# Delta-rule inverse by levels: three of its six product levels multiply four diagonal blocks of 32 by 32 in place of two of 64 by 64

## The reference

```python
kb = k * beta[..., None]
lower = jnp.where(strict, jnp.einsum('nbhcd,nbhsd->nbhcs', kb, k) * decay, 0.0)
eye = jnp.eye(C, dtype=jnp.float32)                       # C = 64
rhs = jnp.concatenate([v * beta[..., None], kb * jnp.exp(gc)[..., None]], axis=-1)
sol = lax.linalg.triangular_solve(eye + lower, rhs, left_side=True, lower=True,
                                  unit_diagonal=True)
```

## Time and profile before

| | us |
|---|---|
| median of the runs (lowest, highest) | 2251.85 (2248.36, 2258.47) |
| the profiled execution, its own time | 2253.49 |
| its span, first instruction to last | 2251.7 |
| TensorE matmul busy | 2146.6 (95%) |
| VectorE busy | 1097.8 (49%) |
| ScalarE busy | 752.4 (33%) |
| mean granted TensorE clock | 0.977 of full |
| the levels of group 0 | about 244 to 276 |
| the levels of group 1 | about 304 to 348 |

### The profile page before, as it was taken

The page is one execution under the profiler, slowest core; times in us unless marked ns, Lnnn a source line. Parts: engine busy times, 40 slices in busy tenths (PEclk is TensorE's granted clock), DMA queues, the critical chain, the costliest instruction groups (busy, mean ns, idle before and its releaser), DMA issues.

```text
span 2251.7 us, 28790 instructions
## 1 busy us (share of the span) xinstructions
PE 2146.6 (95%) x11831; PEld 1757.9 (78%) x11831; DVE 1097.8 (49%) x1381; ACT 752.4 (33%) x1038; POOL 155.3 (7%) x137
## 2 busy tenths in 40 slices
PE   7999999899999999999999999899789999999998
PEld 6877888788888778767788888687469868888886
DVE  4664654454354353452744435555745334454453
ACT  5443432422122232673312213312435243222222
POOL 2000220200000210001100000300001001000001
PEclk9999999999999999999999999999889999999999
DMA  6231000122222222102222222322104302222221
GB/s 233 75 115 45 22 11 15 70 100 98 93 93 93 94 75 75 38 1 75 75 94 105 99 94 93 122 94 75 38 20 143 119 20 94 94 94 99 106 93 56
DMA packets 27025, 182.81 MB, mean 81 GB/s; under 512 B 2992, under 2 KB 3120, under 8 KB 5424
## 3 DMA queue, kind: packets, MB, share of 16 engines
q1 hardware_dynamic: 25200, 174.07, 21.8%
q10 hardware_dynamic: 1296, 4.71, 0.5%
q0 software_dynamic: 432, 2.62, 0.3%
HBM read 179.30 MB, written 2.10 MB: 81 GB/s over the span
## 4 chain that ended last, share of the span: by engine, by line
PE 86%; DVE 8%; ACT 3%; DMA 1%; issue 1%; POOL 0%; ACTq 0%; DVEq 0%; POOLq 0%; SPq 0%
PE PS L472 85%; ACT Y L1254 2%; DVE HL L1888 2%; DVE Y L1888 1%; DVE PS L1888 1%; DVE XT L1891 1%; DVE WL L1891 1%; ACT WH L1254 1%; DVE Y L1891 1%; DMA MX<-mem_t 0%; DVE SQ L1891 0%; PE PS L1070 0%; DMA STG<-weights 0%; PE PS L641 0%; POOL SQA L412 0%
## 5 line engine op out<-in xcount | busy, mean ns | idle before, releaser
L472 PE MATMUL PS<-HH,WH 128*128 128x512 f32 x1608 | 643.0, 400 | 32.4 <-DVE HL L1888 26.0
L472 PE MATMUL PS<-HL,WH 128*128 128x512 f32 x1608 | 632.1, 393 | 0.0
L472 PE MATMUL PS<-HH,WL 128*128 128x512 f32 x1608 | 631.6, 393 | 0.0
L1891 DVE TENSOR_TENSOR WL<-STG,WH 128x2048 fp32r<-128x2048 f32 (+1 forms) x167 | 376.3, 2253 | 286.5 <-ACT WH L1254 286.5
L1254 ACT ACTIVATE WH<-STG 128x2048 fp32r<-128x2048 f32 (+1 forms) x167 | 313.9, 1880 | 529.3 <-PE PS L472 527.8
L472 PEld LDWEIGHTS PS<-HH,WH 128*128 128x128 f32 x1608 | 305.4, 190 | 112.5 <-issue 28.7
L472 PEld LDWEIGHTS PS<-HH,WL 128*128 128x128 f32 x1608 | 305.4, 190 | 65.2
L472 PEld LDWEIGHTS PS<-HL,WH 128*128 128x128 f32 x1608 | 305.8, 190 | 62.7 <-issue 1.7
L472 PE MATMUL PS<-UPH,WH 128*128 128x512 f32 x768 | 299.1, 389 | 1.4 <-DVE UPL L1888 1.4
L472 PE MATMUL PS<-UPL,WH 128*128 128x512 f32 x768 | 298.8, 389 | 0.0
L472 PE MATMUL PS<-UPH,WL 128*128 128x512 f32 x768 | 298.8, 389 | 0.0
(11 more groups left out here) (291 smaller groups left out, 2127.2 us busy)
## 6 DMA issues: line engine op xcount, KB each, us to landing
STG<-weights SPq DMA_DIRECT2D x163, 1024.0 KB, 4.8
XT<-x_t ACTq DMA_DIRECT2D x2, 1024.0 KB, 12.4
out_t<-Y SPq DMA_DIRECT2D x8, 256.0 KB, 2.0
STG<-weights SPq DMA_DIRECT2D x4, 256.0 KB, 5.7
MX<-mem_t ACTq DMA_DIRECT2D x4, 256.0 KB, 8.3
CON<-consts ACTq DMA_DIRECT2D x1, 1024.0 KB, 17.2
Y<-recip_counts POOLq DMA_DIRECT2D x1, 1024.0 KB, 5.1
KVM<-mem_t POOLq DMA_DIRECT2D x1, 1024.0 KB, 7.2
```

Source lines behind the costliest of these rows:

```text
L472: return pe.matmul(o, l, r, start=start, stop=stop, **kw)
L1891: return dve.tensor_tensor(o, a, b, op)
```

## The change

`corners` gets a block size `n` (64 as before, or 32). It walks over the diagonal blocks of `n` partitions and takes the columns of each block alone. For levels 2, 3 and 4 the caller passes 32; levels 1 and 5, and level 0, stay at 64.

```diff
-            def corners(bank, col, a, x=None):
+            def corners(bank, col, a, x=None, n=64):
                 for b in range(NB):
-                    for o in (0, 64):
-                        last = mm(PS[o:o + 64, bank, col + 64 * b:col + 64 * b + 64], blk(a[o:o + 64], b, 64),
-                                  IDC[o:o + 64] if x is None else blk(x[o:o + 64], b, 64), True, True)
+                    for o in range(0, P, n):
+                        c = slice(64 * b + o % 64, 64 * b + o % 64 + n)
+                        last = mm(PS[o:o + n, bank, col + c.start:col + c.stop], a[o:o + n, c],
+                                  IDC[o:o + n] if x is None else x[o:o + n, c], True, True)
                 return last
...
-                            corners(3 + e, 0, BT[e][lv % 2], XX[e] if lv else None).then_inc(sems["lv_y"], 1)
+                            corners(3 + e, 0, BT[e][lv % 2], XX[e] if lv else None, 32 if 2 <= lv < 5 else 64)\
+                                .then_inc(sems["lv_y"], 1)
...
-                            corners(e, 0, XTr[e], YT[e])
-                            corners(e, 256, YT[e], XTr[e]).then_inc(sems["lv_p"], 1)
+                            n = 32 if 2 <= lv < 5 else 64
+                            corners(e, 0, XTr[e], YT[e], n=n)
+                            corners(e, 256, YT[e], XTr[e], n=n).then_inc(sems["lv_p"], 1)
```

## The result

The changed kernel takes 2265.08 us, the median of 20 runs (2257.44 to 2273.37), against 2251.79 us for the kernel before (20 runs, 2246.69 to 2259.26). The ratio is 1.0051, 95% interval 1.0040 to 1.0061: 9 to 14 us slower, near 11.5 (the medians differ by 13.3). The forecast was 2248.5, range 2244 to 2264, with 0.17 on slower by over 0.5%.

What follows compares the result with a forecast made beforehand. In group 0's levels TensorE's and VectorE's lines were both taken as full; in group 1 p products were on the path. Six levels at 0.54 us (3.2) plus 0.2 in level 2 gave 2251.85 - 3.4 = 2248.5 us, range 2244 to 2264.

Steps and rivals of the forecast that it cites:

- whether four places can be fed: In `corners` at 32: whether TensorE can start instructions fast enough for four array places; slower than now above 14.6 ns a start.
- the low bound of the feed's cost is nothing: In `corners` at 32: feeding four places may cost nothing; the high bound was 0.933 us a call.
- Rival 1: Levels 2 to 4: starting twice the instructions is the bound; +7.5 us at 19.5 ns a start, +24 at 29.2; chance 0.22.
- The array's price: In `corners`: a 32-column instruction holds its place 32 to 58.4 ns; 45 ns taken, 0.36 us a call.
- The path: Levels 2 to 4: faster p calls shorten a level by 0.54 us, through VectorE's line in group 0, likewise in group 1.
- my sum: Per level: 0.21 us before the first subtraction plus 0.33 before the next two; six levels 3.2, level 2's y products 0.2.
- Rival 2: In `corners`: a product's two instructions hold up the next product; +2 to +12 us, chance 0.05.
- Rival 3: Levels 2 to 4: TensorE's clock falls to half with the smaller products; +13 us over six levels, chance 0.06.
- one of the two signs: Signs named as proving the forecast wrong: a level over 5.7 us, or a granted clock of 0.5 in levels 2 to 4.
- The level of 5.1 us: Group 0's level, from its first p product to the next level's, was to shrink from 5.66 to about 5.1 us.
- the worst half of the rivals: Slower outcomes left out above the range's upper end of 2264 us; over 0.5% slower had 0.17.

Runs made afterwards that it cites:

- e8_half: The changed kernel with the 32 by 32 products of chunks 2 and 3 left out at levels 2 to 4; ratio 0.9974 to the kernel before.
- e6_order: The changed kernel with its 32 by 32 products reordered, the four chunks of one place one after another; ratio 1.0112 to the kernel before.
- e1_after: The changed kernel run once more without any edit; ratio 1.0058 to the kernel before.
- e3_y32: The changed kernel with p products back at 64, only y products of levels 2 to 4 at 32; ratio 1.0005 to the kernel before.
- e2_p32: The changed kernel with y products back at 64, only p products of levels 2 to 4 at 32; ratio 1.0046 to the kernel before.
- e5_p32_head0: The kernel before with only the first head's p products at 32 in levels 2 to 4, y products at 64; ratio 1.0001 to the kernel before.
- e12_budget_c: The kernel before with 32 at levels 2 to 4 only for group 1's p products of heads 0 and 1 and group 0's first p call of head 0; ratio 0.9993.
- e10_dup32: The changed kernel with the p products of levels 2 to 4 issued twice at 32; ratio 1.0220 to the kernel before.

## Why the prediction was wrong

**The step that failed** is "whether four places can be fed", and in it "the low bound of the feed's cost is nothing", which I took into the sum. I asked how fast TensorE can start instructions and answered from 0.12 us of overtaking. That shows what it does with instructions that it already has. What the runs showed in its place: they come 256 in 3.5 to 3.8 us, and the changed kernel waits 12.4 us for them. The question was how fast they come over a level, and the stretch to read was 5 us long: 308 instructions in 5.66 us at best, which says nothing about 596 in the same time. Rival 1 had the mechanism, "twice as many instructions have to be brought", and even its limit: 14.6 ns a start of 32 matmuls is 7.3 ns an instruction, and the feed gives 14.4. At that pace for every call it priced +24 us; the measured +11.5 is half of that, since TensorE waits only where a block is used up in less than 3.7 us, and the calls between waits gain from the small products. I gave it 0.22. The trace of before had the evidence in its queue q8, whose packets come 3.73 us apart at the closest (265.49, 269.22); the page gives 1.21 MB in 74 packets, 16 KB each, and I did not ask what a packet lasts.

**The array's price** was right at its low end. I took 45 ns for an instruction of 32 columns between 32 and 58; it is 35 (0.28 us a call), near the line through 64 and 128 columns (32). The floor cited from the Trainium skill, page "TensorE: Matmul & The Clock Gate", section "Wait — 56ns, not 53.3ns?" (starts never under about 25 ns apart), is not what this trace shows over several places: starts here are 8.75 ns apart. One place takes a new fp32 instruction every 35 ns, where the estimate from that page was 50.

**The path.** That a faster call shortens a level of group 0 only through VectorE's line was near the mark: e8_half's p call takes about 0.15 us, its level 3 4.45 us (260.15 to 264.60); my sum, with 0.30 for two calls, gives 0.57 + 1.54 + 2.59 = 4.7. In group 1 it is less sure: e8_half gains 3.1 us in group 0 and 1.6 in group 1, where I had put the same for both. With 0.28 a call my sum gives an estimated 4.6 us for the complete change: 0.37 + 0.33 at each of six levels, and 0.4 in level 2's y products. No complete kernel showed that gain, since the wait for instructions outweighed it.

**Rival 2** (a product's instructions hold the next up) fell for the order of the change: four places work at once. e6_order shows a limit of it. **Rival 3** (the clock): it did fall in the levels, one of the two signs that I had named against my forecast, but behind the first stops; e1_after, with another phase of the clock and the same stops, says that it isn't what makes them. What it added to the time is known only for single products (1 us in level 5's y products of group 0). The Trainium skill, page "TensorEngine Tiling (Array Packing)", section "Instruction Overhead", puts some 60 cycles on each matmul, which spoke against the change. The change is slower, but not by a cost of each matmul: a call takes 0.28 us and not the estimated 0.80, and e3_y32 has a third of the small products and pays 0.2 us in the levels.

**What was to show it.** The level of 5.1 us became 8.6, over the 5.7 that I had named as the mark against me. The range missed by 1 us at its upper end, because I left out "the worst half of the rivals" when the likeliest of them had its middle there.

## What to carry to other kernels

Splitting a product into smaller ones has to be paid in instructions. Count TensorE's matmuls and weight loads (its waits too), and see how long each 256 in a row take by the other limits; hold that against what the instruction queue has been seen to bring (here 256 in about 3.7 us). The sum over a whole stage isn't enough, since a slow part stores no more than a block for the quick one (e2_p32, group 1). If a trace has idle time of TensorE that "issue" ends, look at the instruction queue's packets: stops that stand a block apart, at the same instruction in every run, point to starvation. Small products on several places of the array may be worth it where every block stays slower than that; here the kernels that nearly kept to it (e3_y32, e5_p32_head0, e12_budget_c) neither lost nor gained anything that the time could tell.

## What the runs showed of the hardware

- TensorE's instructions come in packets of 16 KB, 256 instructions. A starved TensorE gets one in 3.5 to 4.0 us and goes on 2.2 to 2.9 us after its packet starts (the changed kernel, e1_after, e10_dup32).
- In the changed kernel's group 0 the packet of a block starts only 1.1 to 1.6 us after TensorE has entered the block before it.
- Four 32 by 32 places on the diagonal work fully side by side: 0.28 us for 32 fp32 instructions, 35 ns each in its place.
- With the four products of a place issued in a row a call takes 0.61 us, as if fewer than two places worked at once (e6_order). That TensorE looks ahead over other places' instructions only so far would explain it; how far is not shown.
- In the changed kernel TensorE's clock went from 2.4 to 1.2 GHz at the end of the stop of 2.46 us (257.90 to 260.30 idle at 1.00, then 0.50).
